# A two-block transformer kernel: in the second block's attention, selected keys become the first softmax group, compressed keys the third

## The chip, the cores and the metric

The kernel runs on one core of a Trainium2 chip. The time is device microseconds of one launch, the median of several runs. Engines are named as in the profile: PE is TensorE (matmuls, and transposes, which are matmuls with an identity), PEld its weight loads, DVE is VectorE, ACT is ScalarE, POOL is GpSimd and SP is SyncE, whose queue (SPq) issues nearly all weight loads. All data is f32.

## The reference

The reference runs a first block (two layers of mixer and mixture of experts) and then a second block of two layers on 256 tokens, width 1024. The change touches the attention of the second block alone. Each of its layers computes, cut to what matters:

```python
proj = h @ w_in[l]                       # q_a, k_c, v_c, k_s, v_s, k_w, v_w, g_a, c_q, c_kv, k_r
k_cmp = _compress(_rope(k_c), cmp_pos_k[l], cmp_w1_k[l], cmp_w2_k[l])   # silu(flat @ w1) @ w2
v_cmp = _compress(v_c, cmp_pos_v[l], cmp_w1_v[l], cmp_w2_v[l])          # 15 blocks, 2 groups
o_a = g[..., 0] * o_cmp + g[..., 1] * o_sel + g[..., 2] * o_win         # three softmax branches
o_b = _mla(c_q, c_kv, k_r, ...)                                         # causal attention, 8 heads
mixed = concat([_rms_norm(o_a), _rms_norm(o_b)])
x = x + mixed @ w_out[l]
x = x + square(relu(_rms_norm(x) @ w_ff1[l])) @ w_ff2[l]
```

With 256 tokens every block of keys is selected, so the selected branch is plain causal attention. The window is 512 wide, so that branch is causal attention too, over other keys and values. The compressed branch has only 15 keys per group.

## The kernel before

Each engine has its own instruction list, and semaphores order them. A layer of the second block is, on PE, `norm`, `project2`, `compress`, `attention`, `output`, `norm`, `mlp`.

**The end of project2.** PE multiplies the blocks of keys and values by the first compression weights (L2422). ACT turns the product into `hid` with Silu (L611), PE transposes the last window keys, and ACT copies them into `kSD` (L583). That copy is the last thing that PE waits for before it goes on.

**compress.** PE transposes `hid` (L2433, two small transposes); DVE copies the result into `hidT` and `hv` (L1697 and L1701, five copies); PE makes the compressed keys and values (L2441 and L2443, four products); DVE copies them into `kC` (L1707) and the block-diagonal `vBD` (L1708). The banks are the shared ones of psum, handed over by `mm_v` and `v_free`. Then attention starts.

**attention.** `groups_2` lists 11 groups of heads per layer. For query tile m = 0 (128 keys) they are compressed (8 heads x 16 columns), selected, window, MLA (8 heads x 128 keys each). For m = 1 (256 keys) they are compressed, and then two groups of 4 heads each of selected, window and MLA. Below, group 0 is the first of the list and group 10 the last. Every group passes through the same steps:

- `scores(n)` on PE (L1966): one product for each head; the records count two matmuls for each.
- `maxima(n)` on DVE: add the mask (L1080), take the row maxima (L1082), scale them (L1085).
- `exps(n)` on ACT (L663): one exponential for each head, with its sum.
- `turn(n)` on PE (L1825): transpose the probabilities, 8 blocks (1 for a compressed group).
- the evacuation: half by ACT (L672; L675 is its stand-in for a compressed group), half by DVE (L1097).
- `values(n)` on PE (L1991; L1988 for a compressed group).
- `output(n)` on DVE: reciprocal (L1108), for compressed groups a factor `keep` (L1113), the gate (L1119), and then the product. The group that is `first` of its three branches writes the result directly (L1129; MLA by L1133); the others write a product (L1123) and add it (L1126).

The order on the engines is written out by hand. PE does scores(0), and then for each n: scores(n+1), values(n-1), turn(n). DVE does maxima(0), and then for each n: maxima(n+1), the evacuation of n, output(n-1). ACT does exps(0), and then for each n: the evacuation of n, exps(n+1). At its beginning PE's attention waits until all banks are free:

```python
pe.wait_ge(v_free, v_done.value())
pe.wait_ge(a_free, a_done.value())
```

After attention, `rms_rows` on DVE and POOL normalises the rows; only then does PE go on with `output`, and then with the MLP. The weights of both come by SP's queue.

Of the kernel before, what the change touches and what calls it, by code (L numbers as in the profile page):

```python
# [10 lines left out]
P = 128  # L11
# [6 lines left out]
HD = 64  # L18
# [8 lines left out]
SCALE = HD ** -0.5  # L27
# [129 lines left out]
def build(nc, t):  # L157
# [7 lines left out]
    with ctx:  # L165
# [3 lines left out]
        def sem(name):  # L169
            return ctx.enter_context(nc.semaphore(name))  # L170
# [142 lines left out]
        x_fetched = [sem(f"x_fetched{b}") for b in range(2)]  # L313
        diag_ready = sem("diag_ready")
        kv_turned = sem("kv_turned")
        rounds_ready = sem("rounds_ready")


# [42 lines left out]
        def groups_2():  # L361

            out = []
            for m in (0, 1):
                nk = P * (m + 1)
                def half(x, h):
                    return x[64 * (h % 2):64 * (h % 2) + 64]

                q = [half(qT2, h)[:, h // 2, P * m:P * m + P] for h in range(8)]
                parted = [0, 2, 4, 6, 1, 3, 5, 7]  # L370
                out.append(dict(nk=16, heads=parted, mask=(0, co("cmp_add", at=16 * m, width=16)), sink=None, dv=HD, scale=SCALE,
                                scores=[(q[h], half(kC, h)[:, h // 4, :]) for h in parted], pv_all=vBD, parted=True,
                                gate=(m, 0), keep=co("cmp_keep", at=16 * m, width=1), out=oA[:, m, 0:512], first=True))
                for kind in ("sel", "win", "mla"):
                    w = 0 if kind == "sel" else 1
                    for h0 in range(0, 8, 1024 // nk):
                        hs = list(range(h0, h0 + 1024 // nk))[:8]
                        g = dict(nk=nk, heads=hs, mask=(P * m, co("causal")), sink=None, dv=HD)
                        if kind != "mla":
                            hs = hs[0::2] + hs[1::2]  # L380
                            g.update(heads=hs, parted=True)
                        if kind == "mla":
                            g.update(scale=MLA_SCALE, out=oA[:, m, 512 + HD * h0:512 + HD * (hs[-1] + 1)],
                                     scores=[(qM[0:MLA_D, h, P * m:P * m + P], kM[0:MLA_D, h, 0:nk]) for h in hs],
                                     pv=[[VM[:, b, HD * h:HD * h + HD] for b in range(m + 1)] for h in hs])
                        else:
                            v0 = VW2 if w else VS2
                            g.update(scale=SCALE, out=oA[:, m, HD * h0:HD * (h0 + len(hs))], gate=(m, 1 + w), first=False,
                                     scores=[(q[h], half(kSD, h)[:, w, h // 4, 0:nk]) for h in hs],
                                     pv=[[PR[:, b, v0 + HD * (h // 4):v0 + HD * (h // 4) + HD] for b in range(m + 1)] for h in hs])  # L390
                        out.append(g)
            return out
# [461 lines left out]
        def _(dve):  # L854
# [7 lines left out]
            def so_far(sem):  # L862

                return own.setdefault(sem.name, Tally(sem)).next()

            def next_bank():

                job[0] += 1
                return psum[:, (job[0] - 1) % 4, :]
# [187 lines left out]
                        dve.wait_ge(rows_ready, so_far(rows_ready))  # L1057
                        j += 1

            def attention(groups):  # L1060
# [39 lines left out]
                def output(g):  # L1100
# [31 lines left out]
                    else:  # L1132
                        dve.tensor_tensor(g["out"].rearrange("p (u n) -> p u n", u=heads), o,  # L1133
                                     rden[:, b, 0:heads, None].to_broadcast([P, heads, dv]), ALU.mult).then_inc(att_o, 1)
                        dve.wait_ge(att_o, so_far(att_o))

                maxima(groups[0])
                for n in range(len(groups)):
                    if n + 1 < len(groups):
                        maxima(groups[n + 1])  # L1140
                    evac(groups[n])
                    if n:
                        output(groups[n - 1])
# [546 lines left out]
                window(1)  # L1690
                chunks.n += 4

            def compress():
                dve.wait_ge(mm_v, jobs.next())
                bank = next_bank()
                t4 = bank[:, 0:P].rearrange("p (j s n) -> p s j n", j=2, s=2)
# [5 lines left out]
                inst.then_inc(v_free, 1)  # L1702
                dve.wait_ge(v_free, so_far(v_free))
                dve.wait_ge(mm_v, jobs.next())
                bank = next_bank()
                kc = bank[:, 0:30].rearrange("p (g i) -> p g i", g=2)
                dve.tensor_copy(kC[:, :, 0:15], kc)  # L1707
                dve.tensor_tensor(vBD, bank[:, None, 64:128].to_broadcast([P, 8, HD]),  # L1708
                                  co("block_diag")[:, :, None].to_broadcast([P, 8, HD]), ALU.mult).then_inc(v_free, 1)
                dve.wait_ge(v_free, so_far(v_free))  # L1710

            def mlp():
                for c in range(8):
# [63 lines left out]
            for l in range(DEPTH):  # L1777
                scalers(2)
                turned2(G_ATTN + KB * l)
                project2(l)  # L1780
                compress()
                attention(groups_2())
# [10 lines left out]
        def _(pe):  # L1793
# [152 lines left out]

            att_n = [0]

            def attention(groups):
# [5 lines left out]
                def scores(n):  # L1955
                    g = groups[n]
                    if base + n >= 2:
                        pe.wait_ge(att_e, base + n - 1)
                    s = psum[:, 2 * ((base + n) % 2):2 * ((base + n) % 2) + 2, :].rearrange("p a n -> p (a n)")
                    order = range(len(g["scores"]))  # L1960
                    if g.get("parted"):
                        order = [u for pair in zip(order[:len(order) // 2], order[len(order) // 2:]) for u in pair]
                    for u in order:
                        q, k = g["scores"][u]
                        at = score_at(g, u)
                        inst = pe.matmul(s[:, at:at + g["nk"]], q, k, start=True, stop=True)  # L1966
                    inst.then_inc(att_s, 1)
# [25 lines left out]
                    inst.then_inc(att_pv, 1)  # L1993

                scores(0)
                for n in range(len(groups)):
                    if n + 1 < len(groups):
                        scores(n + 1)
                    if n:
                        values(n - 1)  # L2000
                    turn(n)
# [423 lines left out]
                            inst.then_inc(used, 1)  # L2425
                window_T(1)

            def compress():
                pe.wait_ge(a_free, a_done.value())
                pe.wait_ge(v_free, v_done.value(back=3))  # L2430
                bank = v_bank()
                for j in range(2):
                    inst = pe.transpose(bank[:, 64 * j:64 * j + 62], hid[0:62, P * j:P * j + P], ident[0:62, 0:62])  # L2433
                inst.then_inc(mm_v, 1)
                pe.wait_ge(v_free, v_done.value())
                pe.wait_ge(v_free, v_done.value(back=3))
                bank = v_bank()
                k2 = pa("cmp_w2k", at=256 * layer[0], width=256).rearrange("p (j n) -> p j n", j=2)
                v2 = pa("cmp_w2v", at=P * layer[0], width=P).rearrange("p (j n) -> p j n", j=2)
# [4 lines left out]
                inst.then_inc(mm_v, 1)  # L2444
                layer[0] += 1

            layer = [0]

            def mlp():

# [61 lines left out]
            for l in range(DEPTH):  # L2512
                norm(2)
                project2()
                compress()
                attention(groups_2())
                output([2, 3], 2)
                norm(2)
                mlp()
# [200 lines left out]
```

## Time and profile before

| | us |
|---|---|
| median of 3 runs | 2573.7 (2572.71 to 2574.23) |
| the profiled execution, its own time | 2578.21 |
| its span | 2575.9 |
| PE busy in the span | 2342.6 (91%) |
| DVE busy | 855.6 (33%) |
| ACT busy | 392.6 (15%) |
| attention with compress, first layer (1815.75 to 1876.12) | 60.37 |
| attention with compress, second layer (2232.48 to 2287.49) | 55.01 |

The span is cut into stretches by the time from its start. The granted clock (PEclk) is given in parts of full speed: 1.00 is 2.4 GHz, 0.50 is 1.2 GHz, and a value between is a stretch in which both occurred. A row of the timeline or of the chain gives the start, the duration, the engine, the line of the kernel and the number of instructions that were merged. In square brackets is the idle time before, and what ended it.

### The profile page before, as it was taken

How to read it: one execution, taken by the hardware profiler on the slowest of the kernel's cores; microseconds unless marked ns; L12 is line 12 of the kernel's file. 1: busy time of each engine (PE TensorE's matmuls, PEld its weight loads, DVE VectorE, ACT ScalarE, POOL GpSimd, SP SyncE). 2: the span in 40 equal slices, each digit the busy share in tenths (PEclk: the TensorE clock that was granted, in tenths of full speed). 3: DMA queues.
4: the chain of work that ended last, by engine and by line, in shares of the span. 5: the costliest groups of instructions: out<-in, count | busy, mean ns of one | idle time of the engine just before them, and what ended most of it. 6: DMA issues, size and time to landing. Idle time of an engine off the chain costs nothing.

```text
span 2575.9 us, 27680 instructions
## 1 busy us (share of the span) xinstructions
PE 2342.6 (91%) x10290; PEld 1239.4 (48%) x10290; DVE 855.6 (33%) x1717; ACT 392.6 (15%) x958; POOL 83.1 (3%) x104
## 2 busy tenths in 40 slices
PE   5889788999999969997899999989879999979998
PEld 2336336333333334444544444435748744657843
DVE  2557423333333355453222222234620002551101
ACT  1006202010001010041101110111510001331000
POOL 0110001000000002101000000000000000000000
PEclk9999898999999989998899999999879999989999
DMA  9563624999999952203599999983223443403441
GB/s 360 182 229 153 229 80 178 421 421 421 421 422 421 421 214 75 81 8 114 221 422 422 422 422 422 422 342 114 99 66 131 163 147 112 166 18 114 163 151 69
DMA packets 148929, 609.32 MB, mean 237 GB/s; under 512 B 9584, under 2 KB 21872, under 8 KB 99568
## 3 DMA queue, kind: packets, MB, share of 16 engines
q1 hardware_dynamic: 145072, 592.94, 58.9%
q10 hardware_dynamic: 2480, 10.10, 1.0%
q0 software_dynamic: 1296, 5.17, 0.5%
q8 instruction: 54, 0.88, 0.1%
q14 instruction: 27, 0.22, 0.0%
HBM read 594.02 MB, written 14.16 MB: 236 GB/s over the span
## 4 chain that ended last, share of the span: by engine, by line
PE 75%; DVE 10%; DMA 7%; issue 3%; ACT 2%; POOL 1%; SPq 1%; DVEq 0%; ACTq 0%; POOLq 0%
PE psum L2255 16%; PE psum L1890 11%; PE psum L2465 9%; PE psum L2478 9%; PE psum L2268 7%; PE psum L2315 6%; PE psum L2348 4%; PE psum L1825 4%; DMA rows<-in_w 3%; DMA ring<-in_w 3%; PE psum L1882 2%; PE psum L2229 1%; POOL rstd L427 1%; PE psum L2019 1%; PE psum L2058 1%
## 5 line engine op out<-in xcount | busy, mean ns | idle before, releaser
L2255 PE MATMUL psum<-ring,arena 128*64 128x512 f32 x1536 | 345.1, 596 | 5.6 <-issue 2.2
L1890 PE MATMUL psum<-ring,hT 128*128 128x512 f32 x640 | 282.2, 600 | 3.6 <-issue 1.6
L1483 DVE TENSOR_TENSOR arena<-arena,psum 128x512 f32<-128x512 f32 x204 | 140.3, 688 | 289.5 <-PE psum L2268 289.5
L2478 PE MATMUL psum<-ring,arena 128*128 128x512 f32 x512 | 220.3, 592 | 3.2 <-DVE arena L1719 3.2
L2465 PE MATMUL psum<-hT,ring 128*128 128x256 f32 x1024 | 221.5, 379 | 1.3 <-DVE hT L1564 1.3
L2255 PEld LDWEIGHTS psum<-ring,arena 128*64 128x64 f32 x1536 | 110.7, 137 | 232.0 <-issue 214.4
L2465 PEld LDWEIGHTS psum<-hT,ring 128*128 128x128 f32 x1024 | 194.4, 190 | 28.0 <-DVE hT L1564 1.7
L1890 PEld LDWEIGHTS psum<-ring,hT 128*128 128x128 f32 x640 | 121.9, 193 | 153.9 <-issue 150.8
L2268 PE MATMUL psum<-arena 128*128 128x512 f32 x408 | 184.2, 601 | 1.7 <-DVE arena L1546 1.7
L2315 PE MATMUL psum<-ring,arena 128*64 128x512 f32 x768 | 171.9, 596 | 7.1 <-DVE arena L1534 7.1
L2478 PEld LDWEIGHTS psum<-ring,arena 128*128 128x128 f32 x512 | 97.1, 190 | 125.5 <-issue 121.5
L1825 PE MATMUL psum<-con,arena 128*128 128x128 f32 (+1 forms) x832 | 123.2, 287 | 24.8 <-DVE mark L910 11.3
L1825 PEld LDWEIGHTS psum<-con,arena 128*128 128x128 f32 (+1 forms) x832 | 96.0, 146 | 74.6 <-issue 21.9
L2268 PEld LDWEIGHTS psum<-arena 128*128 128x128 f32 x408 | 74.7, 190 | 110.8 <-issue 107.3
L2255 PE MATMUL psum<-rows,arena 128*64 128x512 f32 x512 | 115.7, 593 | 3.0 <-DMA rows<-in_w 3.0
L782 ACT ACTIVATE arena<-psum 128x512 f32<-128x512 f32 x68 | 40.6, 597 | 471.1 <-PE psum L2229 244.5
L1882 PE MATMUL psum<-scaler,X 128*128 128x128 f32 x352 | 57.2, 341 | 55.6 <-DVE scaler L947 55.6
L2315 PEld LDWEIGHTS psum<-ring,arena 128*64 128x64 f32 x768 | 55.9, 137 | 101.3 <-issue 96.7
L1530 DVE TENSOR_TENSOR arena<-psum,arena 128x512 f32<-128x512 f32 x32 | 33.9, 1059 | 206.7 <-PE psum L2255 206.7
L1890 PE MATMUL psum<-arena,hT 128*128 128x512 f32 x192 | 89.1, 620 | 13.0 <-DVE mod_sum L917 9.4
L2348 PE MATMUL psum<-ring,hT 128*128 128x512 f32 (+2 forms) x256 | 94.7, 525 | 4.0 <-DVE gate L1653 2.6
L425 POOL TENSOR_SCALAR rstd<-sumsq 128x8 f32<-128x8 f32 (+2 forms) x43 | 15.4, 358 | 2432.0 <-ACT rows L509 1812.0
(286 smaller groups left out, 2158.4 us busy)
## 6 DMA issues: line engine op xcount, KB each, us to landing
ring<-in_w SPq DMA_DIRECT2D x288, 1024.0 KB, 11.3
rows<-in_w SPq DMA_DIRECT2D x96, 1024.0 KB, 12.8
ring<-in_w_ff SPq DMA_DIRECT2D x64, 1024.0 KB, 5.2
ring<-in_w_mod SPq DMA_DIRECT2D x40, 1024.0 KB, 13.8
ring<-in_w_in_c SPq DMA_DIRECT2D x12, 1024.0 KB, 7.1
x_rows<-arena ACTq DMA_DIRECT2D x1, 8704.0 KB, 33.1
gate<-in_w_mod SPq DMA_DIRECT2D x8, 1024.0 KB, 15.1
hT<-x_rows SPq DMA_DIRECT2D x16, 512.0 KB, 15.9
```

The source lines that it names most:

```text
L782: act.activation(xgT[:, b, 4 * h:4 * h + 4, :], psum[:, 5 + h, :].rearrange("p (k n) -> p k n", k=4), ACT.Copy).then_inc(a_free, 1)
L1483: dve.tensor_tensor(f, f, bank, ALU.add).then_inc(v_free, 1)
L1530: dve.tensor_tensor(act_by_quarter, quarters(bank), quarters(siluG), ALU.mult).then_inc(v_free, 1)
L1825: return pe.transpose(out, in_, ident)
L1882: inst = pe.matmul(bank[:, P * m:P * m + P], X[:, 4 - nt + m, P * k:P * k + P], scaler[:, m, :], start=True, stop=True)
L1890: inst = pe.matmul(bank, hT[:, k, P * m:P * m + P], w[k], start=k == 0, stop=k == KB - 1)
L2255: inst = pe.matmul(out[64 * e:64 * e + 64, :], xgT[:, b, k, 64 * e:64 * e + 64], m, start=k == 0, stop=k == KB - 1)
L2268: pe.matmul(bank, shareT[:, m, :], ySlot[:, 512 * h:512 * h + 512], start=True, stop=True).then_inc(mm_v, 1)
L2315: inst = pe.matmul(outs[h][64 * e:64 * e + 64, :], actT[:, f, 64 * e:64 * e + 64], m, start=f == 0, stop=f == 3)
L2348: inst = pe.matmul(bank[:, 0:n], hT[:, k, P * m:P * m + P], w[k // 4][:, k % 4, :], start=k == 0, stop=k == KB - 1)
L2465: inst = pe.matmul(bank[:, SEQ * f:SEQ * f + SEQ], w[k][:, at:at + P], hT[:, k, 0:SEQ], start=k == 0, stop=k == KB - 1)
L2478: inst = pe.matmul(banks[2 * m + h], aT[:, 2 * c + f, P * m:P * m + P], w[:, f, 512 * h:512 * h + 512], start=c == 0 and f == 0, stop=c == ...
```

## The change

`compress` goes. Its two PE steps become `hidden_T` and `compressed` inside PE's attention: `hidden_T` behind scores(0), `compressed` behind scores(1). They use banks 6 and 7 of psum (those of the values, which are not yet in use) and semaphores of their own, `cmp_turned` and `cmp_taken`. DVE copies into `hidT` and `hv` ahead of maxima(0), and makes `kC` and `vBD` between maxima(0) and maxima(1). PE waits for `kC` and `vBD` once, ahead of scores(2). The list of groups is now selected, window, compressed, MLA for m = 0, and two selected, two window, compressed, two MLA for m = 1. Selected groups are now `first` (they write directly), and the compressed ones add.

```diff
-                out.append(dict(nk=16, heads=parted, mask=(0, co("cmp_add", at=16 * m, width=16)), sink=None, dv=HD, scale=SCALE,
...
+                cmp = dict(nk=16, heads=parted, mask=(0, co("cmp_add", at=16 * m, width=16)), sink=None, dv=HD, scale=SCALE,
...
+                           gate=(m, 0), keep=co("cmp_keep", at=16 * m, width=1), out=oA[:, m, 0:512], first=False)
                 for kind in ("sel", "win", "mla"):
+                    if kind == "mla":
+                        out.append(cmp)
...
-                            g.update(scale=SCALE, out=oA[:, m, HD * h0:HD * (h0 + len(hs))], gate=(m, 1 + w), first=False,
+                            g.update(scale=SCALE, out=oA[:, m, HD * h0:HD * (h0 + len(hs))], gate=(m, 1 + w), first=kind == "sel",
 # DVE, attention
+                hidden_taken(l)
                 maxima(groups[0])
+                compressed(l)
                 for n in range(len(groups)):
 # DVE, the two halves of what was compress
+            def hidden_taken(l):
+                dve.wait_ge(cmp_turned, 2 * l + 1)
+                t4 = psum[:, 6, 0:P].rearrange("p (j s n) -> p s j n", j=2, s=2)
                 dve.tensor_copy(hidT[:, 0:2, 0:30], t4[:, 0, :, 0:30])
...
+                inst.then_inc(cmp_taken, 1)
+            def compressed(l):
+                dve.wait_ge(cmp_turned, 2 * l + 2)
+                bank = psum[:, 7, :]
...
+                                  co("block_diag")[:, :, None].to_broadcast([P, 8, HD]), ALU.mult).then_inc(cmp_taken, 1)
 # PE, attention
                 scores(0)
+                hidden_T()
                 for n in range(len(groups)):
+                    if n == 1:
+                        pe.wait_ge(cmp_taken, 2 * l + 2)
                     if n + 1 < len(groups):
                         scores(n + 1)
+                    if n == 0:
+                        compressed(l)
                     if n:
                         values(n - 1)
                     turn(n)
 # PE, the two halves
+            def hidden_T():
+                for j in range(2):
+                    inst = pe.transpose(psum[:, 6, 64 * j:64 * j + 62], hid[0:62, P * j:P * j + P], ident[0:62, 0:62])
+                inst.then_inc(cmp_turned, 1)
+            def compressed(l):
+                pe.wait_ge(cmp_taken, 2 * l + 1)
+                bank = psum[:, 7, :]
...
+                inst.then_inc(cmp_turned, 1)
```

## Rows read from the trace of the kernel before

**Rows 1.** The page: the span, and the chain that ended last by engine.
```profile
span 2575.9 us, 27680 instructions
...
PE 75%; DVE 10%; DMA 7%; issue 3%; ACT 2%; POOL 1%; SPq 1%; DVEq 0%; ACTq 0%; POOLq 0%
```

**Rows 2.** Windows, both attentions, four stretches each; columns as in the second line.
```profile
core 0: us, PE busy (x) PEld busy (x) DVE busy (x) ACT busy (x) POOL busy (x), PEclk, DMA share, GB/s
1815.75:1826.23 10.48, 7.35 (x53) 6.51 (x55) 4.97 (x14) 3.61 (x19) 0.00 (x0) 0.58 0.83 308
1826.23:1839.55 13.32, 12.44 (x92) 10.13 (x88) 10.64 (x20) 9.88 (x50) 0.00 (x0) 0.82 0.01 2
1839.55:1866.95 27.40, 24.21 (x179) 20.31 (x179) 24.59 (x49) 16.05 (x65) 0.00 (x0) 1.00 0.01 1
1866.95:1876.12 9.17, 7.57 (x40) 6.99 (x40) 3.07 (x9) 2.07 (x9) 0.00 (x0) 0.59 0.00 0
2232.48:2241.13 8.65, 5.02 (x49) 4.24 (x51) 4.97 (x14) 3.61 (x19) 0.00 (x0) 0.78 1.02 378
2241.13:2253.63 12.50, 11.70 (x96) 9.79 (x93) 10.63 (x20) 9.88 (x50) 0.00 (x0) 0.88 0.01 4
2253.63:2281.02 27.39, 24.20 (x179) 20.30 (x179) 24.61 (x49) 16.05 (x65) 0.00 (x0) 1.00 0.00 1
2281.02:2287.49 6.47, 4.88 (x40) 4.50 (x40) 3.07 (x9) 2.07 (x9) 0.00 (x0) 1.00 0.00 0
```

**Rows 3.** The chain of waits, second layer, from the hidden transposes on.
```profile
2232.48 0.35 PE psum L2433 x2
...
2232.92 0.22 DVE arena L1697
2233.14 0.52 DVE gate L1701 x4
...
2233.70 0.63 PE psum L2441 x4
...
2235.10 0.61 DVE arena L1708
```

**Rows 4.** Timeline, second layer: scores and maxima of the selected group at m = 0.
```profile
2236.67 1.55 PE L1966 MATMUL psum<-arena 64*128 64x128 f32 x16
...
2238.33 1.23 DVE L1080 TENSOR_TENSOR psum<-psum,con 128x1024 f32<-128x1024 f32 x1 [0.56 <-PE psum L1966]
```

**Rows 5.** The chain of waits, second layer, groups 2 and 3.
```profile
2245.95 2.91 ACT arena L663 x16
...
2248.90 1.11 PE psum L1825 x8
...
2250.09 0.60 ACT arena L672
```

**Rows 6.** Timeline, DVE, second layer: pieces of group 3 and later.
```profile
2254.87 0.69 DVE L1097 COPY arena<-psum 128x512 f32<-128x512 f32 x1 [1.17 <-PE psum L1825]
...
2257.49 0.70 DVE L1080 TENSOR_TENSOR psum<-psum,con 128x512 f32<-128x512 f32 x1
...
2259.68 0.29 DVE L1097 COPY arena<-psum 128x128 f32<-128x128 f32 x1
...
2268.66 0.42 DVE L1123 TENSOR_TENSOR rows<-psum,rden 128x256 f32<-128x256 f32 x1
...
2280.28 0.69 DVE L1097 COPY arena<-psum 128x512 f32<-128x512 f32 x1
```

**Rows 7.** Timeline, PE: scores of MLA at m = 0, values, transposes; full and half clock.
```profile
1829.18 1.97 PE L1825 MATMUL psum<-con,arena 128*128 128x128 f32 x8
...
1871.70 3.67 PE L1991 MATMUL psum<-gate,arena 128*128 128x64 f32 x16 [0.85 <-DVE arena L1097]
...
2245.06 1.95 PE L1966 MATMUL psum<-gate,arena 96*128 96x128 f32 x16
...
2250.99 2.00 PE L1991 MATMUL psum<-arena 128*128 128x64 f32 x16
```

More of the change, by code:

```diff
@@ L315, in build @@
         kv_turned = sem("kv_turned")
+        cmp_turned, cmp_taken = sem("cmp_turned"), sem("cmp_taken")
         rounds_ready = sem("rounds_ready")
@@ L370, in groups_2 @@
                 parted = [0, 2, 4, 6, 1, 3, 5, 7]
-                out.append(dict(nk=16, heads=parted, mask=(0, co("cmp_add", at=16 * m, width=16)), sink=None, dv=HD, scale=SCALE,
-                                scores=[(q[h], half(kC, h)[:, h // 4, :]) for h in parted], pv_all=vBD, parted=True,
-                                gate=(m, 0), keep=co("cmp_keep", at=16 * m, width=1), out=oA[:, m, 0:512], first=True))
+                cmp = dict(nk=16, heads=parted, mask=(0, co("cmp_add", at=16 * m, width=16)), sink=None, dv=HD, scale=SCALE,
+                           scores=[(q[h], half(kC, h)[:, h // 4, :]) for h in parted], pv_all=vBD, parted=True,
+                           gate=(m, 0), keep=co("cmp_keep", at=16 * m, width=1), out=oA[:, m, 0:512], first=False)
                 for kind in ("sel", "win", "mla"):
+                    if kind == "mla":
+                        out.append(cmp)
                     w = 0 if kind == "sel" else 1
@@ L1058, in heads_c, with attention @@
                         j += 1
-            def attention(groups):
+            def attention(l, groups):
                 def maxima(g):
@@ L1691, in project2 @@
                 chunks.n += 4
[L1693 to L1696, printed above, removed]
+            def hidden_taken(l):
+                dve.wait_ge(cmp_turned, 2 * l + 1)
+                t4 = psum[:, 6, 0:P].rearrange("p (j s n) -> p s j n", j=2, s=2)
                 dve.tensor_copy(hidT[:, 0:2, 0:30], t4[:, 0, :, 0:30])
@@ L1701, in compress @@
                         inst = dve.tensor_copy(hv[:, j, 4 * s:4 * s + 4, 0:15].rearrange("p (g h) i -> p g h i", g=2), src)
[L1702 to L1705, printed above, removed]
+                inst.then_inc(cmp_taken, 1)
+            def compressed(l):
+                dve.wait_ge(cmp_turned, 2 * l + 2)
+                bank = psum[:, 7, :]
                 kc = bank[:, 0:30].rearrange("p (g i) -> p g i", g=2)
@@ L1708, in compress @@
                 dve.tensor_tensor(vBD, bank[:, None, 64:128].to_broadcast([P, 8, HD]),
-                                  co("block_diag")[:, :, None].to_broadcast([P, 8, HD]), ALU.mult).then_inc(v_free, 1)
-                dve.wait_ge(v_free, so_far(v_free))
+                                  co("block_diag")[:, :, None].to_broadcast([P, 8, HD]), ALU.mult).then_inc(cmp_taken, 1)
             def mlp():
@@ L1780, in _ @@
                 project2(l)
-                compress()
-                attention(groups_2())
+                attention(l, groups_2())
                 rms_rows(2, [rows[:, 2, :], rows[:, 3, :]])
@@ L1947, in _, with attention @@
             att_n = [0]
-            def attention(groups):
+            def attention(l, groups):
                 pe.wait_ge(v_free, v_done.value())
@@ L2426, in project2 @@
                 window_T(1)
[L2428 to L2431, printed above, removed]
+            def hidden_T():
                 for j in range(2):
[L2433 to L2439, printed above, removed]
+                    inst = pe.transpose(psum[:, 6, 64 * j:64 * j + 62], hid[0:62, P * j:P * j + P], ident[0:62, 0:62])
[3 more added lines that the diff above has]
+                bank = psum[:, 7, :]
+                k2 = pa("cmp_w2k", at=256 * l, width=256).rearrange("p (j n) -> p j n", j=2)
+                v2 = pa("cmp_w2v", at=P * l, width=P).rearrange("p (j n) -> p j n", j=2)
                 for j in range(2):
@@ L2443, in compress @@
                     inst = pe.matmul(bank[:, 64:128], hv[:, j].rearrange("p h n -> p (h n)"), v2[:, j, :], start=j == 0, stop=j == 1)
-                inst.then_inc(mm_v, 1)
-                layer[0] += 1
-            layer = [0]
+                inst.then_inc(cmp_turned, 1)
             def mlp():
@@ L2514, in _ @@
                 project2()
-                compress()
-                attention(groups_2())
+                attention(l, groups_2())
                 output([2, 3], 2)
```

## The prediction

> **What bounds the kernel now.** I read the page first: PE holds three quarters of the chain that ended last, DVE a tenth [rows 1]. That is an average. So I went to the windows of the two attentions [rows 2]. Each attention has four stretches. The head runs from the transposes of `hid` to the first exponential of the selected group. Then comes tile 0, up to the end of MLA's exponentials. The body of tile 1 runs to the last group but one, and the tail follows. The first layer takes 10.48 + 13.32 + 27.40 + 9.17 = 60.37 us, the second 8.65 + 12.50 + 27.39 + 6.47 = 55.01 us. The bodies are the same; the layers differ where the granted clock fell: 0.58, 0.82 and 0.59 in the first layer's head, tile 0 and tail, against 0.78, 0.88 and 1.00 in the second's.
>
> Each stretch has its own bound. In the head it is a dialogue of PE and DVE: transposes 0.35, copies 0.22 and 0.52, products from 2233.70, `kC` and `vBD` until 2235.71 [rows 3], and only then the first scores. In tile 0 the bound is ACT: exponentials 2.91, transposes 1.11, copy 0.60, from 2245.95 to 2250.72, a period of 4.77 [rows 5]. In tile 1 it is DVE: from 2254.87 to 2280.97 it works 26.1 us in a row [rows 6]. These are the cycles in which the compressed groups now find room: in the head, group 0's softmax runs on ACT while DVE makes the selected maxima. The change moves that group to a place where room must be found anew.
>
> The sum is made for the second layer, whose clock is the cleaner, counted from 2232.48, and then carried to the first.
>
> **The head after.** PE makes the selected scores first. The row has 1.55, with some of it at half clock [rows 4, 2]; if all of it had been, 0.78 is left as the lower bound, and MLA's scores, 1.95 [rows 7], are the upper; I take 1.55, the row of this very operation. Then the transposes of `hid`, 0.35, and a hand-over of about 0.1. DVE copies for 0.74 (0.22 + 0.52) [rows 3]. Its maxima, up to ACT's start, take 2.80 (2238.33 to 2241.13) [rows 4, 2]. That makes 1.55 + 0.35 + 0.09 + 0.74 + 2.80 = 5.53, against 8.65: 3.1 us saved in the second layer. In the first it is 10.48 - 5.53 = 4.95. Window's scores and the four compression products run on PE beside DVE's work. `kC` and `vBD` (0.8, of which 0.61 in [rows 3]) run on DVE while ACT makes the first exponentials (2.91), followed by window's maxima (2.80): 3.6 against ACT's and PE's 2.91 + 1.11 + 0.60 = 4.62 before ACT wants the next bias, so they are hidden; without this cover they would cost 0.8. The wait for `cmp_taken` ahead of scores(2) holds the second values and turns behind it, but it ends before the first exponentials do: nothing.
>
> **Tile 0 after.** Call the start of the first exponentials x. Window's start at x + 4.77, and its transposes end at x + 4.77 + 2.91 + 1.15 = x + 8.83. Before, one more period gave MLA's start. Now the compressed exponentials stand there, on ACT, but MLA's must wait for MLA's maxima, and DVE makes these only after the evacuation of window's transposes and the output of selected: 0.04 + 0.72 + 1.17 + 2.80 = 4.73. The 1.17 is reciprocal, gate and one product: 2254.87 to 2257.49, 2.62, less the evacuation and the addition, 0.72 each [rows 6], since selected no longer adds. PE is nearly as late: MLA's scores 1.95 and window's values 2.00 [rows 7] come before the compressed group's small transpose, over 4.0 in all. So MLA's exponentials start at x + 13.6 and end at x + 16.5, against 12.50 [rows 2] before: 4.0 us given back. The compressed exponentials are no longer than the 2.91 of the others, and so cover neither the 4.7 of DVE nor the 4 of PE. Bounds: nothing, if something hid it all (a rival below), and one whole period of 4.77.
>
> **Tile 1 after.** MLA's transposes end about 1.15 after its exponentials; DVE comes some 0.2 later than now, since the selected maxima (2.19, [rows 6], 2257.49 to 2259.68) and window's output stand ahead of the evacuation. In the 26.1 us in a row there are now six wide maxima, then five and one compressed. That one is put at 0.9, three steps at the 0.29 of the 128-wide copy in [rows 6] (estimate): -1.3. The outputs: both selected groups lose their addition (2 x 0.46, by the 256-wide 0.42 of [rows 6] and its hand-over). Tile 0's compressed output, with `keep` and now an addition, comes in where window's was (+0.3), and tile 1's moves out behind the stretch, where the last values hide it, with one of window's moving in (-0.1). That is -0.8 (estimate, from 2.62 less 0.72 for a wide output). But PE is now late once. After the compressed maxima DVE has nothing until window's second transposes: values 2.00 and transposes 1.11 [rows 7, 5] against an output of 0.87 and maxima of 0.9: +1.4. Together 0.2 - 1.3 - 0.8 + 1.4 = -0.5; without that cover missing it is -1.9, which is the lower bound, and with the additions as before +0.3, the upper. The tail ends in two MLA groups in both orders: the same 6.47.
>
> **The layers.** Second: 5.53 + 16.5 + (27.39 + 6.47 - 0.5 = 33.4) = 55.4, against 55.01: +0.4. First: 5.53 + 16.5 + (27.40 + 9.17 - 0.5 = 36.1) = 58.1, against 60.37: -2.3.
>
> **The clock.** Before, the clock was low in both heads after PE's short pieces with pauses. After the change PE works for about 1.55 + 0.35 + 1.55 + 1.1 = 4.6 us without a stop, and then idles until the first exponentials end at 5.53 + 2.91 = 8.4: 3.8 us with nothing to do, the longest pause of the attention. I expect the low level there. What it costs on the path is the first turn: 1.97 instead of 1.11 [rows 7, 5], +0.9 a layer; the values behind it (3.67 instead of 2.00) lie beside ACT's exponentials. As the scores may be quicker than 1.55 by up to 0.8, I count 0.4 a layer net. That gives +0.8 and -1.9, in sum **-1.1 us**.
>
> The page "TensorE: Matmul & The Clock Gate" of the Trainium skill, section "HAM oscillation — how this bites in real kernels", warns of just such pauses: each lets the array fall back to half rate, and the next burst starts cold. Rows 2 agree that the clock falls in the attention's thin stretches. By that rule alone each layer would lose the 0.9 again, and the sum would be near 0 in place of -1.1. It speaks against the change, and is the mechanism of the third rival.
>
> Of moved work, nothing issues a DMA, and no wait of SP or POOL is passed. The products give up no `used`, so the weight loads are released as before. After attention all is the same, but the moment at which PE leaves half clock in `output` can shift. PE there is the bound, so this costs or gives up to 1.7 us a layer (one turn at half clock more or less; estimate from the 3.67 against 2.00 of [rows 7]). I count it as nothing, and into the range.
>
> The profiled execution has its own time of 2578.21 and a span of 2575.9; the median of the runs is 4.5 below the former. The sum of -1.1 us is taken off the median: 2573.7 - 1.1 = **2572.6**. A measurement of this kernel can tell about 0.2%, 5.1 us, from no change.
>
> **Rivals.**
>
> 1. *The head's gain is kept.* The third place costs nothing: tile 0 stays at 12.50, and the layers become 5.53 + 12.50 + 36.1 = 54.1 (-6.3) and 5.53 + 12.50 + 33.4 = 51.4 (-3.6), in sum -9.9: 2563.8. For it: ACT has less than one period of work for the group. Against: MLA's maxima follow scores that PE makes only after window's turn, and DVE is behind as well. Chance 0.06.
> 2. *The first layer also loses its slow tail.* PE's clock in the tail is 0.59 in one layer and 1.00 in the other with the same instructions, so it hangs on timing, and the change moves this. Then 9.17 becomes 6.47: a further -2.7, and -3.8 in sum: 2569.9; with quicker scores or a warm first turn (0.5 a layer) 2568.9. Chance 0.2.
> 3. *Slower: the pause lets the clock stay low through tile 0.* Then PE, not ACT, sets the period: scores about 2, values 3.67, transposes 1.97 [rows 7], 7.7 against 4.77, +2.9 for each of two periods. Second layer 55.4 + 5.9 = 61.3 (+6.3), first 58.1 + 5.9 = 64.0 (+3.6): +9.9, 2583.6. It decides from two periods in one layer and one in the other on (+6.3 and +0.7, 2580.7); one period in each gives +4.0, 2577.7, still inside 0.2%. For it: the first layer's tile 0 had 0.82. Against: PE is busy for 0.93 to 0.94 of the stretch there [rows 2], and got the full clock back each time. Chance 0.07.
> 4. *Nothing starts earlier*, because PE's wait at the start of attention still holds for the last window keys, and the head is paid elsewhere: 2573.7 to 2575. This is inside the forecast's own range. Chance 0.05.
>
> **How the numbers follow.** The forecast, 2572.6, has 0.62; its own range is 2570.3 to 2575.5 (those 1.7 either way, and the 0.8 and 1.9 by which the first scores and tile 1 are open). The rest is as above: 0.06, 0.2, 0.07 and 0.05. Eight in ten reach from 2568.8, the far end of rival 2, to 2576.3: -1.1, one period of rival 3 (+2.9) and half of the 1.7 of `output`. Faster by over 0.2% (under 2568.6): rival 1 and a little of rival 2, 0.09. Slower by over 0.2% (over 2578.8): most of rival 3, 0.06. Within: 0.85.
>
> **What would show it.** Right: the first exponentials of 128 columns start 5 to 6 us after the last window keys are copied; the start of MLA's exponentials at tile 0 lies 13 to 14 us behind that; PE's scores of group 3 end before DVE makes their maxima, with ACT idle for 1 us or more in front of its MLA exponentials; DVE idles once in the middle of tile 1 for over 1 us; granted clock under 1 at the first turn. Wrong: MLA's start at x + 9.5 to 11 (rival 1); transposes of nearly 2 us in tile 0's second and third turns of both layers (rival 3); an attention whose bodies differ from before by more than 1.5 us, which no step above gives.

## The result, and the profile after

The changed kernel takes 2586.4 us against 2575.0 us for the kernel before (medians of 12 runs each). The ratio is 1.0041, with an interval of 1.0028 to 1.0054: the change costs 7 to 14 us. I had forecast 2572.6, from a median of 2573.7 for the kernel before.

The windows of both attentions after the change, cut like [rows 2]: head, tile 0, body of tile 1, tail; columns in the first line.

```profile
core 0: us, PE busy (x) PEld busy (x) DVE busy (x) ACT busy (x) POOL busy (x), PEclk, DMA share, GB/s
1813.62:1818.49 4.87, 3.24 (x42) 3.00 (x42) 3.26 (x8) 1.29 (x2) 0.00 (x0) 1.00 1.05 388
1818.49:1838.87 20.38, 15.61 (x92) 13.85 (x93) 12.04 (x23) 12.24 (x67) 0.00 (x0) 0.75 0.19 71
1838.87:1866.84 27.97, 25.13 (x194) 21.68 (x195) 24.94 (x52) 17.52 (x71) 0.00 (x0) 0.98 0.01 1
1866.84:1876.01 9.17, 7.56 (x35) 6.96 (x34) 2.69 (x7) 0.60 (x1) 0.00 (x0) 0.50 0.00 0
2233.21:2238.03 4.82, 3.24 (x42) 3.00 (x42) 3.27 (x9) 1.29 (x3) 0.00 (x0) 0.98 1.05 391
2238.03:2258.55 20.52, 15.76 (x92) 13.99 (x93) 12.05 (x23) 12.24 (x67) 0.00 (x0) 0.67 0.21 77
2258.55:2286.39 27.84, 25.00 (x194) 21.54 (x195) 24.80 (x52) 17.42 (x71) 0.00 (x0) 0.99 0.01 2
2286.39:2295.56 9.17, 7.55 (x35) 6.96 (x34) 2.83 (x7) 0.70 (x3) 0.00 (x0) 0.50 0.00 0
```

| us (granted clock) | head | tile 0 | tile 1, body and tail | attention |
|---|---|---|---|---|
| before, first layer | 10.48 (0.58) | 13.32 (0.82) | 36.57 (1.00, 0.59) | 60.4 |
| after, first layer | 4.87 (1.00) | 20.38 (0.75) | 37.14 (0.98, 0.50) | 62.4 |
| before, second layer | 8.65 (0.78) | 12.50 (0.88) | 33.86 (1.00, 1.00) | 55.0 |
| after, second layer | 4.82 (0.98) | 20.52 (0.67) | 37.01 (0.99, 0.50) | 62.3 |
| forecast, first layer | 5.53 | 16.5 | 36.1 | 58.1 |
| forecast, second layer | 5.53 | 16.5 | 33.4 | 55.4 |

The head gained more than I had said, 5.6 and 3.8 us. Tile 0 gave back 7.1 and 8.0, where I had said 4.0. In the second layer tile 1 lost 3.2 as well. In both places the granted clock moved: 0.75 and 0.67 in tile 0, where [rows 2] have 0.82 and 0.88, and 0.50 (1.2 GHz) in a tail that [rows 2] show at 1.00 in the second layer.

Timeline of PE after the change, second layer, from the selected scores to MLA's scores.

```profile
2233.31 1.16 PE L1971 MATMUL psum<-arena 64*128 64x128 f32 x16 [0.52 <-issue]
...
2235.91 0.64 PE L2453 MATMUL psum<-par,gate 128*128 128x64 f32 x4
2240.98 1.97 PE L1830 MATMUL psum<-con,arena 128*128 128x128 f32 x8 [4.43 <-ACT arena L666]
2242.88 1.89 PE L1971 MATMUL psum<-gate,arena 64*128 64x16 f32 x16
2244.70 3.67 PE L1996 MATMUL psum<-arena 128*128 128x64 f32 x16
2248.17 1.91 PE L1830 MATMUL psum<-con,arena 128*128 128x128 f32 x8
2249.87 2.75 PE L1971 MATMUL psum<-gate,arena 96*128 96x128 f32 x16
```

PE finishes the compression products at 2236.55 and then has nothing for 4.43 us, until ACT ends the first exponentials. Then everything runs at the lower level: transposes 1.97 against 1.11 [rows 5], scores of 16 columns 1.89, values 3.67 against 2.00 [rows 7], transposes again 1.91. Only within MLA's scores does the clock come back, so that the values behind them take 1.90. ACT, which set the pace before, shows the price.

Timeline of ACT, same stretch. The number in brackets is its idle time before the row.

```profile
2238.03 0.37 ACT L666 ACTIVATE arena<-psum,nbias 128x128 f32<-128x128 f32 x1 [3.52 <-DVE nbias L1088]
...
2243.04 0.60 ACT L675 ACTIVATE arena<-psum 128x512 f32<-128x512 f32 x1 [2.12 <-PE psum L1830]
2243.67 0.37 ACT L666 ACTIVATE arena<-psum,nbias 128x128 f32<-128x128 f32 x1
...
2250.18 0.60 ACT L675 ACTIVATE arena<-psum 128x512 f32<-128x512 f32 x1 [3.61 <-PE psum L1830]
2250.81 0.27 ACT L666 ACTIVATE arena<-psum,nbias 128x16 f32<-128x16 f32 x1
...
2255.52 0.37 ACT L666 ACTIVATE arena<-psum,nbias 128x128 f32<-128x128 f32 x1 [0.75 <-DVE nbias L1088]
```

The exponentials of selected start at 2238.03, those of window at 2243.67, the compressed ones at 2250.81 and MLA's at 2255.52. The second period is 7.14 us, where it was 4.77 [rows 5]. ACT waits 3.61 us for the second turn: it stood behind the cold values on PE. The third period is 4.71. The forecast has 4.1 for it: its 4.73 is counted from the end of window's transposes, and the copy of 0.60 lies between that end and the compressed exponentials. The rest is MLA's cold scores, which end at 2252.62, just ahead of the maxima that MLA's exponentials wait for.

Timeline of PE in the tail, second layer: turn, values, turn, values.

```profile
2282.69 1.09 PE L1830 MATMUL psum<-con,arena 128*128 128x128 f32 x8 [0.24 <-ACT arena L666]
2285.24 3.32 PE L1996 MATMUL psum<-gate,arena 128*128 128x64 f32 x16 [1.46 <-DVE arena L1100]
2288.35 1.91 PE L1830 MATMUL psum<-con,arena 128*128 128x128 f32 x8
2291.12 3.68 PE L1996 MATMUL psum<-gate,arena 128*128 128x64 f32 x16 [0.85 <-DVE arena L1100]
```

The values before the last and the last take 3.32 and 3.68 and the turn between them 1.91. At full clock the values take 2.00 [rows 7] and a turn 1.0 to 1.1. The last values but one already start cold, behind pauses of 0.24 and 1.46 us.

### The profile page after: what moved, and what is told of

Read it like the earlier page. It is cut to its first block, busy times and chain, and to the rows that moved or that the text cites. A ratio compares the mean times of both kernels' runs of the same rounds, so it can differ in the third digit from the quotient of the medians.

```text
span 2582.7 us, 27672 instructions
## 1 busy us (share of the span) xinstructions
PE 2345.5 (91%) x10290; PEld 1244.2 (48%) x10290; DVE 854.8 (33%) x1715; ACT 392.6 (15%) x958; POOL 83.1 (3%) x104
## 4 chain that ended last, share of the span: by engine, by line
PE 75%; DVE 10%; DMA 8%; issue 3%; POOL 1%; ACT 1%; SPq 1%; DVEq 0%; ACTq 0%; POOLq 0%
PE psum L2265 16%; PE psum L1895 11%; PE psum L2473 9%; PE psum L2486 9%; PE psum L2278 7%; PE psum L2325 5%; PE psum L1830 4%; PE psum L2358 4%; DMA rows<-in_w 3%; DMA ring<-in_w 3%; PE psum L1887 2%; PE psum L1996 1%; POOL rstd L430 1%; PE psum L2239 1%; PE psum L2029 1%
## 5 line engine op out<-in xcount | busy, mean ns | idle before, releaser
L1535 DVE TENSOR_TENSOR arena<-psum,arena 128x512 f32<-128x512 f32 x32 | 33.9, 1060 | 206.7 <-PE psum L2265 206.7
```

The costliest lines, as they stand in the source:

```text
L1535: dve.tensor_tensor(act_by_quarter, quarters(bank), quarters(siluG), ALU.mult).then_inc(v_free, 1)
```

## Experiments

Two theories stood against each other. The *clock theory*: the new order opens pauses on PE, the clock falls in them, and the work behind them is paid at half speed. The *order theory*: the compressed groups stand at a dearer place, and the clock is only a symptom. Most kernels below fill a pause: PE transposes the identity into a bank of psum that nobody reads at that time, so that it stays at work and, if the fill is short enough, starts its next step no later. Nothing that is computed changes. Medians are of 6 to 12 runs (more of the kernel before), and come from four sets of runs, in which the kernel before had 2575.0, 2574.1, 2577.0 and 2574.2, so kernels are compared by their ratios to it.

```python
def fill(n, bank):
    for j in range(n):
        transpose(psum[:, bank, 256:384], ident)
```

**The head's pause filled.** The changed kernel, with one line:

```diff
                     if n == 0:
                         compressed(l)
+                        fill(28, 5)
```

> The changed kernel, with 28 transposes of the identity (nobody reads them) in PE's pause between the compression products and the first turn. Clock theory: the pause in the head lets the clock fall, and it stays low through two turns and one set of values; with the pause filled, the first turns take 1.1 us in place of 1.97, the values 2.0 in place of 3.67, and the attention from the last key copy to the last output shrinks from 62 to about 58.5 us a layer: 2579 in place of 2586. Order theory: the time was lost because the compressed groups stand at a dearer place; filling changes nothing or holds PE up, 2586 to 2588, and MLA at tile 0 still starts 17 us after the first exponentials.

Measured: 2576.4 us, ratio to the kernel before 1.0008 (0.9998 to 1.0017), against 1.0041. That is about 8.5 us less than the changed kernel. The expectation had 58.5 us for each attention; the trace has 59.3 and 59.0. Windows of its second layer: head, tile 0, body, tail.

```profile
2227.62:2232.45 4.83, 4.72 (x58) 4.62 (x59) 3.27 (x9) 1.30 (x3) 0.00 (x0) 1.00 1.05 395
2232.45:2249.10 16.65, 12.60 (x107) 10.63 (x106) 12.05 (x23) 12.27 (x67) 0.00 (x0) 1.00 0.23 84
2249.10:2277.44 28.34, 26.59 (x194) 22.59 (x195) 24.83 (x52) 17.48 (x71) 0.00 (x0) 0.92 0.00 1
2277.44:2286.64 9.20, 7.59 (x35) 7.00 (x34) 2.78 (x7) 0.66 (x2) 0.00 (x0) 0.50 0.00 0
```

Tile 0 is at 1.00 and takes 16.65 us. The forecast's working at full clock had 16.5. The tail is still at 0.50. The order theory is out for tile 0: same order, 3.9 us less. The timeline of ACT says where the 3.9 had gone. Starts of window's, the compressed and MLA's exponentials, with the fill:

```profile
2237.22 0.37 ACT L666 ACTIVATE arena<-psum,nbias 128x128 f32<-128x128 f32 x1
...
2242.00 0.27 ACT L666 ACTIVATE arena<-psum,nbias 128x16 f32<-128x16 f32 x1
...
2246.07 0.37 ACT L666 ACTIVATE arena<-psum,nbias 128x128 f32<-128x128 f32 x1 [0.85 <-DVE nbias L1088]
```

From 2232.45 on the periods are 4.77, 4.78 and 4.07 us, and MLA starts 13.62 us behind the first exponentials. Without the fill they were 5.64, 7.14 and 4.71. The differences are 0.87 for the first turn, 2.36 for the second turn, which comes late behind cold scores and values, and 0.64 for MLA's cold scores: 3.87 together, the whole of 20.52 less 16.65. The first turn starts 2.95 us behind the first exponential in both kernels, so the fill held nothing up.

**Head and tail filled.** In addition:

```diff
                     turn(n)
+                    if n >= len(groups) - 2:
+                        fill(8, 2 * ((base + n) % 2))
```

> As the kernel with the head's pause filled, and 8 more such transposes behind each of the last two turns, where PE waits for the evacuation. Clock theory: the tail's last values and turn go from 3.67 and 1.9 us to 2.0 and 1.1, another 4 us a layer: about 2571, no slower than the kernel before. Order theory: 2586 or above, since PE gets more to do in front of the last values.

Measured: 2567.4 us, ratio 0.9970 (0.9959 to 0.9981), faster than the kernel before. Second layer, same windows:

```profile
2221.89:2226.71 4.82, 4.72 (x57) 4.62 (x58) 3.27 (x8) 1.28 (x2) 0.00 (x0) 1.00 1.05 393
2226.71:2243.34 16.63, 12.59 (x107) 10.63 (x106) 12.05 (x23) 12.24 (x67) 0.00 (x0) 1.00 0.23 84
2243.34:2267.31 23.97, 22.75 (x179) 19.54 (x179) 21.18 (x45) 14.89 (x62) 0.00 (x0) 1.00 0.00 1
2267.31:2276.51 9.20, 7.70 (x64) 7.11 (x64) 6.44 (x14) 3.23 (x12) 0.00 (x0) 1.00 0.01 2
```

4.82 + 16.63 + 33.17 = 54.6 us, where the sum at full clock had said 55.4. The first layer of this execution had 58.5: its tile 0 was cold again (19.99 us, clock 0.68) although the head was filled. Both layers still had pauses of 1.37 us ahead of the first turn and 0.75 ahead of the second. Turns of PE, first layer, first and second; second layer, second:

```profile
1816.36 1.09 PE L1830 MATMUL psum<-con,arena 128*128 128x128 f32 x8 [1.37 <-ACT arena L666]
...
1821.13 1.97 PE L1830 MATMUL psum<-con,arena 128*128 128x128 f32 x8 [0.75 <-ACT arena L666]
...
2234.43 1.09 PE L1830 MATMUL psum<-con,arena 128*128 128x128 f32 x8 [0.75 <-ACT arena L666]
```

The same turn behind the same pause is cold in one layer and at full clock in the other.

**The order alone.** The kernel before, with the compression in front of attention, and the new list of groups (selected groups are `first`, as in the change):

```diff
-                out.append(dict(nk=16, heads=parted, ... first=True))
+                cmp = dict(nk=16, heads=parted, ... first=False)
                 for kind in ("sel", "win", "mla"):
+                    if kind == "mla":
+                        out.append(cmp)
...
```

> The kernel before, with the new order of groups alone: the compression is made in front of attention as before. Order theory: the whole loss of 10 us and more shows, since the head's gain of 3 us a layer is gone too: 2590 or above. Clock theory: the order costs 2.3 us a layer at full clock (sum of durations), and the rest hangs on where the clock falls; with the first pause now in another place, 2579 to 2587.

Measured: 2589.9 us, ratio 1.0053 (1.0041 to 1.0065). PE in its second layer, from the first turn on:

```profile
2246.17 1.97 PE L1827 MATMUL psum<-con,arena 128*128 128x128 f32 x8 [4.91 <-ACT arena L665]
2248.07 1.89 PE L1968 MATMUL psum<-gate,arena 64*128 64x16 f32 x16
2249.89 3.67 PE L1993 MATMUL psum<-arena 128*128 128x64 f32 x16
2253.36 1.91 PE L1827 MATMUL psum<-con,arena 128*128 128x128 f32 x8
```

The pause is there, 4.91 us (4.10 in the first layer), and so are the cold turns; tile 0 took 20.6 and 20.9 us. So the pause is made by the order (a group of 128-column heads comes first, and PE has nothing more to do once window's scores are made), not by placing the small products among the scores. The median is at the edge of what the order theory expected (2590 or above) and 3 us above the clock theory's range. That range had counted on another pause; with the pause as it is, and both stretches cold, the attentions of this trace come to 66.2 and 65.8 us. So this run tells where the pause comes from, and by itself speaks no less for the order theory.

**Tile 1 in its old order.** The changed kernel, but for m = 1 the compressed group comes first and is `first`:

```diff
+                if m:
+                    out.append(cmp)
                 for kind in ("sel", "win", "mla"):
-                    if kind == "mla":
+                    if kind == "mla" and not m:
                         out.append(cmp)
...
```

> The changed kernel, with tile 1 in its old order (compressed first, then selected, window, MLA); tile 0 and the head as changed. If tile 1's new order is what costs (the late turn behind the compressed group): 2580 or below. By the clock theory tile 1's order is worth no more than 1 us a layer, in either direction, unless the tail's clock is kept: 2584 to 2588, with the tail's granted clock telling which.

Measured: 2585.1 us, ratio 1.0039 (1.0026 to 1.0053), no different from the changed kernel. Its tail, second layer:

```profile
2287.63 2.00 PE L1998 MATMUL psum<-gate,arena 128*128 128x64 f32 x16 [1.19 <-DVE arena L1102]
2289.47 1.74 PE L1832 MATMUL psum<-con,arena 128*128 128x128 f32 x8
2292.06 3.68 PE L1998 MATMUL psum<-gate,arena 128*128 128x64 f32 x16 [0.85 <-DVE arena L1102]
```

With the old order of tile 1 the tail still goes cold, only later: the values before the last are at full speed. So the order of tile 1 is not what costs, within the 5 us or so that the two intervals leave together.

**The kernel before, filled.** 5 transposes behind those of `hid`, 5 behind the compression products, 10 behind scores(1), and 8 + 8 in the tail.

> The kernel before, with its own pauses filled in the same way: 5 + 5 + 10 transposes in the head, 8 + 8 in the tail. It asks what the change is worth once the clock is the same. Clock theory: both orders are within 1 us a layer of each other at full clock (sum of durations 54 to 55 us each), so this kernel lands beside the changed one with both pauses filled, 2565 to 2569. Order theory: it beats that kernel by several us, 2562 or below, since the old order is the better one.

Measured: 2569.4 us, ratio 0.9969 (0.9956 to 0.9982). The changed kernel with head and tail filled had 0.9970. With the pauses filled the change is worth nothing, in either direction, to within about 0.2%. The two attentions took 56.2 and 56.4 us here. Their heads were still at a clock of 0.81 and took 9.0 and 9.1 us, so that this fill did not bring the old order to full clock everywhere, and in the second layer, whose head had taken 8.65, it gained nothing there.

**Only the tail filled**, in the changed kernel.

> The changed kernel with only the tail filled (8 + 8), the head's pause left open. Clock theory: the first turns stay cold (tile 0 at 20 us), the tail is warm (rest 33.3 instead of 37.1): 3.8 us a layer less than the changed kernel, 2577 to 2579. If head and tail were one effect, the tail's fill alone would give nothing, 2586.

Measured: 2579.3 us, ratio 1.0007 (0.9995 to 1.0020). Tile 0 stayed at 20.7 and 20.6 us, tile 1 came down to 33.8 and 33.9. The head's pause and the tail are two separate losses, each about 0.33 to 0.34% of the kernel.

**Only the tail, and only the head, in the kernel before.** These two ask how much of each loss was already there.

> The kernel before, with the tail alone filled (8 + 8). How much of the tail's clock did the kernel before lose by itself? In its trace one layer of two had the cold tail. If that is typical, it gains 3 to 5 us (2571 on 2575), about half of the 8.8 us that the same fill gave the changed kernel, and the change then costs about 4 us through the tail. If before loses the tail as often as after, it gains 8 to 9 us and the tail is not part of the change's cost.

> The kernel before, with the head alone filled (5 + 5 + 10). Before's head lost 1.8 us to the clock in one layer and had about 0.6 in the other, with tile 0 about 1: a gain of 2 to 4 us, against the 8.5 us that filling the head gave the changed kernel. If it gains as much, 8 us, the head's pause is no new cost of the change.

Measured: the tail's fill gives 0.9986 (0.9976 to 0.9995), the head's fill 0.9989 (0.9978 to 1.0001), in us 3.6 and 2.8; the second is not clear of zero. The same fills gave the changed kernel 8.8 (1.0041 to 1.0007) and 8.5 (1.0041 to 1.0008). The difference is what the change itself lost: 5.2 us in the tail and 5.7 us in the head and tile 0, together 10.9. The measured loss is 0.41% of 2575, 10.6. Each of the two parts is worked out from three ratios and so is uncertain by about 5 us: that both took a share is likely, how large each share is, the runs do not show. The total does not hang on this division; it rests on the two filled kernels, 0.9970 and 0.9969.

The kernel before with its head filled also has, in its first layer, the one attention of the old order at full clock throughout: head, tile 0, and tile 1 in two pieces.

```profile
1806.68:1814.97 8.29, 6.68 (x70) 5.66 (x71) 4.96 (x14) 3.64 (x18) 0.00 (x0) 1.00 1.05 389
1814.97:1827.56 12.59, 10.53 (x97) 9.07 (x94) 10.69 (x20) 9.91 (x50) 0.00 (x0) 1.00 0.01 3
1827.56:1852.13 24.57, 22.61 (x167) 18.95 (x168) 21.97 (x44) 15.02 (x62) 0.00 (x0) 1.00 0.01 2
1852.13:1861.33 9.20, 6.40 (x54) 5.79 (x53) 5.65 (x13) 3.13 (x10) 0.00 (x0) 1.00 0.00 0
```

That is 54.65 us, against 54.62 for the changed order at full clock. The head is 3.5 us longer, tile 0 is 4.0 shorter, and tile 1 is 0.6 longer.

**The pause of the normalisation filled too.** 36 transposes in the head, and 60 behind the last values, where PE waits 9.3 us for the rows.

> The changed kernel with head (36) and tail (8 + 8) filled, and 60 more transposes behind the last values, in the 9.3 us in which PE waits for the normalisation of the rows. Clock theory: the transposes of the rows behind it take 1.9 to 2.0 us in place of 3.5 to 3.65, and the output products start warm: 2 to 3 us a layer below the kernel with head and tail filled, 2562 to 2564. Order theory says nothing on it; a fill that overruns its pause would cost the excess, 2569 or more.

Measured: 2568.4 us, ratio 0.9965 (0.9953 to 0.9977). That is not told apart from the 0.9970 of the kernel without the 60 and with 28 in the head. In the trace the 60 took 6.72 us, a pause of 2.77 was left, and the 16 transposes behind it still took 3.30 us against 3.65. The expected 2 to 3 us a layer were not found. Tile 0 of the first layer was cold again, 20.01 us, now with only 0.50 us without work ahead of the first turn.

**Five more, behind the first values.**

> The changed kernel with head (36), tail (8 + 8) and the pause of the row normalisation (60) filled, and 5 more transposes behind the first values, since tile 0 of the first layer still went cold with the head filled. Clock theory: both layers have tile 0 at 16.6 us, both attentions near 55: 3.5 us below the kernel without these 5, about 2565. If the cold tile 0 of that layer had another cause, no difference: 2568.4.

Measured: 2564.3 us, ratio 0.9964 (0.9950 to 0.9977). In its trace both layers are warm, tile 0 16.63 us twice, attention 55.4 and 55.3 us. Against the 0.9965 without these 5 the runs show no gain; the one cold layer in the trace of that kernel was not enough to be seen in the median.

**The compressed groups later.** All pauses filled, and both compressed groups in tile 1, one behind the selected groups and one behind the window groups.

```diff
+                late.append(cmp)
                 for kind in ("sel", "win", "mla"):
-                    if kind == "mla":
-                        out.append(cmp)
+                    if m and kind != "sel":
+                        out.append(late.pop(0))
```

> As the kernel with all three pauses filled, and both compressed groups in tile 1, one behind the selected and one behind the window groups, where DVE is the bound and ACT and PE have room. By the sum of durations at full clock tile 0 loses the 4 us of the compressed group and tile 1 gains about 2.6, in all 1.4 us a layer less: 2559 to 2561. If the place of a compressed group costs nothing at full clock, it is equal to the kernel with all pauses filled.

Measured: 2567.4 us, ratio 0.9966 (0.9951 to 0.9981), no gain. Tile 0 fell to 12.57 us, as worked out, but tile 1 rose to 41.4. PE in tile 1, second layer:

```profile
2248.68 1.07 PE L1972 MATMUL psum<-gate,arena 64*128 64x16 f32 x16
2250.55 3.02 PE L1997 MATMUL psum<-arena 128*128 128x64 f32 x16 [0.80 <-DVE arena L1101]
2253.37 1.91 PE L1831 MATMUL psum<-con,arena 128*128 128x128 f32 x8
...
2257.22 3.67 PE L1997 MATMUL psum<-arena 128*128 128x64 f32 x16
```

Again a pause, only 0.80 us, and behind it values at 3.02 and 3.67 and transposes at 1.91. Then 4 + 6 + 4 transposes were put around that place:

> As the kernel with the late compressed groups and three pauses filled, with 4 + 6 + 4 more transposes around its new pause in tile 1 (the one in which it went to half clock). Clock theory: the rest comes down from 41.4 to about 38 us a layer, so each attention takes 55 or less: 2561 to 2563, the best of all. If the late place itself costs the 4 us, nothing changes: 2567.

Measured: 2564.2 us, ratio 0.9963 (0.9949 to 0.9977). Second layer: head, tile 0, tile 1 in one.

```profile
2224.98:2229.80 4.82, 4.72 (x57) 4.62 (x58) 3.27 (x8) 1.28 (x2) 0.00 (x0) 1.00 1.05 390
2229.80:2242.44 12.64, 11.46 (x100) 10.54 (x99) 10.13 (x15) 9.89 (x50) 0.00 (x0) 1.00 0.33 119
2242.44:2278.61 36.17, 34.76 (x281) 30.11 (x282) 29.54 (x66) 20.48 (x89) 0.00 (x0) 1.00 0.00 1
```

4.82 + 12.64 + 36.17 = 53.6 us, the shortest attention of all kernels here, at full clock throughout. It is 1.7 us a layer below the kernel with everything filled in the order of the change (55.3), and 1.0 below that order's shortest (54.6), where the sum had promised 1.4. The medians do not tell the two kernels apart. They beat the kernel before by 0.36% and 0.37%, and the changed kernel by 0.77% and 0.78%.

## Why the prediction was wrong

**What bounds each stretch** was right. Head: PE and DVE in turns; tile 0: ACT, and after the change once DVE; tile 1: DVE.

**The head after**, 5.53 us, was 4.82 to 4.87. The selected scores took 1.16 in place of 1.55, at full clock; the rest is overlap, since the transposes of `hid` ran in part beside the scores. The small work was hidden as said.

**Tile 0 after**, 16.5 us, is right at full clock: 16.65 with the pause filled, and MLA's exponentials start at x + 13.62, where the sum had x + 13.6.

**Tile 1 after**, 33.4 us in all, is right at full clock: 33.2 and 33.7 with head and tail filled.

**The clock** is the step that failed, in three sentences of it.

1. "What it costs on the path is the first turn: 1.97 instead of 1.11 [rows 7, 5], +0.9 a layer; the values behind it (3.67 instead of 2.00) lie beside ACT's exponentials." The pause I had named was there, 4.43 us for the 3.8 worked out. The first turn cost 0.87, as said. But the cold stretch as a whole cost 3.7 and 3.9 us, not 0.9. What failed is that the values lie beside ACT's exponentials: on PE the second turn stands behind the scores and the values, in order. Cold, these are 1.97 + 1.89 + 3.67 less overlaps = 7.2 from turn to turn (2240.98 to 2248.17), longer than ACT's 2.91 and 0.60 with the turn between them. PE became the bound for one period (2.36 in the second layer), and MLA's cold scores took the rest (0.64). This is rival 3, to which I gave 0.07. It had 2.9 for a cold period and held for one in each layer. For that case it gave 2577.7, still far below the 2586.4 measured, because it had no loss in the tail.
2. "As the scores may be quicker than 1.55 by up to 0.8, I count 0.4 a layer net." The scores were quicker, by 0.4. But this gain was set against a cost of which only the first instruction had been priced.
3. "The tail ends in two MLA groups in both orders: the same 6.47." It was 9.17 in both layers. I had seen the two levels in [rows 2], as rival 2, and only let them fall in the change's favour. No rival had a tail that goes cold. The experiments put this part at 5.2 us of the loss, give or take 5.

So the order itself is worth nothing once the pauses are filled (0.9970 for the changed kernel, 0.9969 for the old one), close to the +0.4 us that the sum gave the second layer. The -2.3 of the first layer counted the cold stretches of the old head and tile 0 as saved and put only 0.4 of new ones against them. Measured is +11.4 us in place of -1.1, and the loss is gone in the filled kernels, so the error is the clock's. The measured 2586.4 is near rival 3's 2583.6 by luck: that sum had two cold periods in each layer and no cold tail that was new, and the runs show little more than one cold period and the tails.

The Trainium skill, "TensorE: Matmul & The Clock Gate", section "HAM oscillation — how this bites in real kernels", says that such a wait throttles the array again and that the next burst starts cold. I had weighed this as a loss of 0.9 a layer. The traces agree on the mechanism: tile 0 was at 0.67 after 4.43 us of nothing, and at 1.00 with the pause filled. The size came from this kernel's own order of waits.

**The signs** that I had set spoke early. The second turns of both layers took 1.92 and 1.91 us, the sign of rival 3, and MLA's exponentials started 17.5 us behind the first ones in the second layer, where 13 to 14 was the sign of being right. DVE did idle once in the middle of tile 1, for 1.32 us, as said.

**What stays open.** Why the tail is cold more often after the change than before. Six kernels here have a tail without fill, each with one trace of two layers. With the new order of tile 1 (the changed kernel, its head filled, the order alone) all six tails were at 0.50, cold from the last values but one, with 0.24 + 1.46 us without work ahead of them. With the old order (the kernel before, its head filled, tile 1 in its old order) four of six went cold, and later, with 1.19 us ahead of the same values. That fits the longer pause, but both tails of the kernel with tile 1 in its old order were cold and its time was no better, so it is not shown. A cold tail made tile 1 2.7 to 3.8 us longer in either order. Also, the first layer's tile 0 stayed cold in two traces with the head filled (28 and 36 transposes). With the 5 further ones it was at full clock, in one trace, and the medians do not show a gain.

## What to carry to other kernels

Before moving a group to the front of a pipeline, write down PE's longest pause before and after, and price everything on PE between that pause and the next hand-over at half clock, in order, not just its first instruction: here the first turn was 0.87 us of 3.87. Where the same instructions show two clocks in two layers of one trace, count that as a cost that can come as well as go. And try the fill first: a few dozen transposes of the identity in the pauses were worth 0.3% to the old order of this kernel and 0.7% to the new one, while the reordering itself was worth nothing.

## What the runs showed that I had not expected

A fill that left part of the pause open did its work: 28 transposes (3.23 us) left 1.37 us of nothing ahead of the first turn, and that turn was at full clock in both layers. A small pause could be followed by half clock all the same: in the kernel with the late compressed groups the values after 0.80 us without work took 3.02, and the next ones 3.67. And a fill can itself run cold. In the old kernel the 10 transposes behind the selected scores took 2.08 and 2.21 us with head and tail filled. With the head alone filled they took 1.31 in the first layer and 2.03 in the second, behind the same products and the same pauses of 0.19 and 0.39 us.
